# Up projection by two-by-two blocks with seven products in a transformer step on one core

## The chip, the cores and the metric

The kernel runs on one core of a Trainium2 chip. The time is the device time of one execution in microseconds, the median of several runs. TensorE (PE) multiplies, VectorE (DVE) and ScalarE (ACT) do elementwise work, GpSimd (POOL) and SyncE (SP) here only issue DMAs. SP's and ScalarE's DMAs are made by hardware queues, GpSimd's by a software queue; all run on the core's 16 DMA engines.

## What is computed

Two layers of a transformer trunk on 128 context tokens and 512 latent tokens, width 1024, float32. All tokens go through the kernel together as T = 644 columns (128 + 512 and four zero columns that pad the convolutions).

```python
def layer(l, x, cvec, ctx_kv, ang):
    m = (silu(cvec) @ w_mod[l] + b_mod[l])
    sh1, sc1, g1, sh2, sc2, g2 = split(m, 6)
    h = _rmsnorm(x, norm1_g[l]) * (1 + sc1) + sh1
    q, k, v, bg, cg, xc = split(h @ w_in[l], SPLITS)
    ...
    o = _diff_attention(q, k_all, v_all, lam)
    y = _rmsnorm(bg * _dwconv3(cg * xc, conv_w[l]), conv_norm_g[l])
    x = x + g1 * (concatenate([o, y]) @ w_out[l])
    h2 = _rmsnorm(x, norm2_g[l]) * (1 + sc2) + sh2
    a, b = split(_dwconv3(h2 @ w_up[l], ffn_conv_w[l]), 2)   # w_up: 1024 x 5632
    x = x + g2 * ((silu(a) * b) @ w_down[l])                 # w_down: 2816 x 1024
    return x, k, v
```

## The kernel before

Activations are kept transposed, features on the 128 partitions and tokens along the columns. Every large product of float32 values a and w is made of three matmuls at the fast float32r rate: both are split into a high part and the rest (h_hi, h_lo and w_hi, w_lo), and hi x hi, hi x lo and lo x hi are summed in PSUM. A weight unit is loaded by SP into raw (two slots of 2048 elements a partition), ScalarE copies it to w_hi (`split_hi`), VectorE subtracts to w_lo (`split_lo`), and TensorE uses it. The stages of a layer are: q/k/v projection (`qkv_unit`, columns in units of 256, T in tiles of 128 tokens as the stationary operand), gated convolution with the attention in between (`conv_half`), output projection (`out_unit`), and the MLP.

The MLP has 22 gates. A gate is a tile of 128 columns of the first half of w_up and the same of the second (a and b). `up_half` makes one half of the 644 columns (322) of one gate: 8 k tiles x 2 (a, b) x 3 matmuls into two PSUM banks. A gate has four banks, two gates alternate over all eight. `up_post` then takes them: ScalarE copies PSUM to ub and the centre tap to cen (which is tmp), VectorE adds the outer two taps, ScalarE makes silu, VectorE the product gt, ScalarE g_hi, VectorE g_lo. The gates are done in two chunks of 12 and 10 (`CHUNKS`); after each chunk the down projection (`down`) multiplies its gates by the rows of w_down that belong to them and VectorE adds the result to x (`add_to_x`, line 1491). Before the MLP the row sums of squares are made (`stat`), the inverse root is spread over the partitions by TensorE (`spread`), and VectorE and ScalarE make h_hi and h_lo of the normalised x (`norm_part`, `norm_hi`). The first gates follow this k tile by k tile.

The modulation vectors come from `mod_sum` (eight groups of small matmuls on a 1 MB unit of w_mod) and `mod_turn`; they are laid between the other work, where TensorE would wait.

The order on each engine is written out by hand and held by semaphores: each engine runs its own program in order. SP's order of loads is a list (`load_order`) up to the first gates, then loops; each load waits until the slot's last reader is done.

Of the kernel before, what the change touches and what calls it, by code (L numbers as in the profile page):

```python
# [7 lines left out]
F32 = mybir.dt.float32  # L8
# [4 lines left out]
ds = bass.ds  # L13
# [27 lines left out]
B_RMS = [(5, 6), (5, 6), (3, 5)]  # L41
# [8 lines left out]
CHUNKS = [12, 10]  # L50
CH0 = [0, 12]
C_U, O_U = 6, 12
UP_U = [16, 36]
DN_U = [28, 46]
N_SPLIT = 54
SPLIT_SLOT = N_SPLIT // 2
MOD_PRE = 8
MOD_LAYER = 24
RAW_SLOT = (N_SPLIT + MOD_LAYER) // 2
# [3 lines left out]
NORM1, MIXN, NORM2 = NT * KT, 2 * 4, 2 * KT  # L63
NORMED = NORM1 + MIXN + NORM2
# [5 lines left out]
GAP_H = [10] * LAST + [7]  # L70


def load_order(l):

    mod = [("mod", j) for j in range(MOD_LAYER)]
    split = [("split", n) for n in range(UP_U[0] + 2)]
# [4 lines left out]
    if l == LAST:  # L81
        return order + mod[12:14] + split[14:17] + mod[14:16] + split[17:18]
# [8 lines left out]
def raw_of(l, n):  # L91

    if n < UP_U[0] + 2:
        return ORDER[l].index(("split", n))
    if l == LAST:
        return n + MOD_LAYER - 8
    return n + MOD_LAYER - (2 if n < DN_U[0] + 2 else 0)


def mod_raw(l, j):  # L100

    return ORDER[l].index(("mod", j)) if j < MOD_LAYER - 2 else raw_of(l, DN_U[0] + 1) + 1 + j - (MOD_LAYER - 2)


# [8 lines left out]
YT_BANKS = [2, 3, 6, 7, 0, 1, 4, 5, 2, 3]  # L113
YT_WAITS = {0: 4, 4: 7, NT: KT}
# [5 lines left out]
def mod_bank(l, h):  # L120

    return PRE_BANKS[h] if l is None else MOD_BANK
# [5 lines left out]
def hybrid_step(nc, x_prompt, x_sample, cache_k, cache_v, c_sample, c_ctx, w_mod, b_mod, norm1_g, w_in, q_norm_g,  # L128
# [3 lines left out]
    with ctx:  # L132
# [18 lines left out]
        aT = sb("aT", [P, N_KEY])  # L151
# [9 lines left out]
        rope_q = sb("rope_q", [P, 2, 2, 4, HD])  # L161
# [33 lines left out]
        setup = ExitStack()  # L195
# [6 lines left out]
        g_hi = sb("g_hi", [P, CHUNKS[0] * T], F32R, scope=mlp)  # L202
        g_lo = sb("g_lo", [P, CHUNKS[0] * T], F32R, scope=mlp)
# [4 lines left out]
        vrow = sb("vrow", [P, DEPTH, 3, P], scope=setup)  # L208
        crow = sb("crow", [P, P], scope=setup)
# [219 lines left out]
        def _(pe):  # L429
# [111 lines left out]
            for l in range(DEPTH):  # L541
# [5 lines left out]
                def qkv_unit(b, t, c0, signal, follow=False):  # L547
# [13 lines left out]
                    elif signal:  # L561
                        ins.then_inc(qkv_full, 1)
# [1061 lines left out]
```

## Time and profile before

| | |
|---|---|
| median of 3 runs | 1702.11 us (1701.38 to 1702.33) |
| profiled execution | 1700.29 us, span of its instructions 1698.3 us |
| granted TensorE clock, mean | 0.981 |
| TensorE busy | 1650.8 us, 97% |
| VectorE busy | 894.3 us, 53% |
| ScalarE busy | 640.1 us, 38% |
| matmuls | 11763 |
| DMA | 162.75 MB, 95 GB/s over the span |

Matmul times overlap (a matmul's row gives 310 ns while the next starts after 148), so what one costs is read from the distance of starts, or from a window's count. The stages of layer 0 lie at about 53 to 162 us (q/k/v), 162 to 312 (convolution and attention), 312 to 392 (output projection), 392 to 568 (up, 12 gates), 568 to 657 (down), 657 to 800 (up, 10 gates), 800 to 872 (down); layer 1 follows in the same order from 876.

### The profile page before, as it was taken

What the parts mean: (1) busy time and instruction counts of PE and PEld (TensorE: products, weight loads), DVE (VectorE), ACT (ScalarE), POOL (GpSimd) and SP (SyncE); (2) the same over time, 40 slices, a digit from 0 to 9 for tenths busy, and PEclk for the clock granted to TensorE, in tenths of its full rate; (3) what the DMA queues carried; (4) which work ended last, traced back from release to release, by engine and by line L of the source; (5) the groups of instructions that cost most, each with busy time, mean ns of one, the idle gap of its engine ahead of it and who ended that gap; (6) DMA issues with size and microseconds to landing.
All of it is one profiled execution on the core that took longest, in us unless ns stands there. A gap on an engine that the chain in (4) does not pass through costs nothing.

```text
span 1698.3 us, 27158 instructions
## 1 busy us (share of the span) xinstructions
PE 1650.8 (97%) x11763; PEld 1580.6 (93%) x11763; DVE 894.3 (53%) x1484; ACT 640.1 (38%) x1015; POOL 4.7 (0%) x12
## 2 busy tenths in 40 slices
PE   5999999999999999999999999999999999999998
PEld 4799888988999999999989988889899999999998
DVE  4773666636655423554458547675655543255442
ACT  3543454324444312444234444442344431144432
POOL 0000000000000000000000000000000000000000
PEclk7899999998999999999989999999999999999999
DMA  9455110363322323221235531103322212322122
GB/s 329 147 181 178 36 50 26 97 209 93 100 75 63 102 85 89 73 73 37 78 112 174 181 106 50 51 26 124 100 75 75 69 57 75 100 75 75 47 65 76
DMA packets 225799, 162.75 MB, mean 96 GB/s; under 512 B 5456, under 2 KB 223120, under 8 KB 225680
## 3 DMA queue, kind: packets, MB, share of 16 engines
q1 hardware_dynamic: 224192, 158.36, 29.7%
q8 instruction: 93, 1.52, 0.4%
q0 software_dynamic: 640, 2.10, 0.3%
q10 hardware_dynamic: 848, 0.56, 0.1%
q14 instruction: 26, 0.21, 0.0%
HBM read 157.32 MB, written 3.67 MB: 95 GB/s over the span
## 4 chain that ended last, share of the span: by engine, by line
PE 90%; DVE 4%; ACT 2%; DMA 1%; issue 1%; DVEq 1%; SPq 0%; ACTq 0%
PE ps L776 12%; PE ps L777 12%; PE ps L778 12%; PE ps L822 6%; PE ps L823 6%; PE ps L824 6%; PE ps L556 3%; PE ps L558 3%; PE ps L557 3%; PE ps L455 3%; PE ps L437 3%; PE ps L438 3%; PE ps L439 3%; PE ps L713 2%; PE ps L647 2%; PE ps L714 2%
## 5 line engine op out<-in xcount | busy, mean ns | idle before, releaser
L776 PE MATMUL ps<-h_hi,w_hi 128*128 128x322 f32 x1408 | 440.3, 313 | 5.5 <-DVE h_lo L1301 5.4
L777 PE MATMUL ps<-h_lo,w_hi 128*128 128x322 f32 x1408 | 440.0, 312 | 0.0
L778 PE MATMUL ps<-h_hi,w_lo 128*128 128x322 f32 x1408 | 438.5, 311 | 0.0
L1260 DVE TENSOR_TENSOR w_lo<-raw,w_hi 128x2048 fp32r<-128x2048 f32 (+2 forms) x108 | 226.1, 2094 | 275.3 <-ACT w_hi L932 275.3
L932 ACT ACTIVATE w_hi<-raw 128x2048 fp32r<-128x2048 f32 (+2 forms) x108 | 189.8, 1758 | 358.8 <-PE ps L824 198.8
L776 PEld LDWEIGHTS ps<-h_hi,w_hi 128*128 128x128 f32 x1408 | 267.1, 190 | 6.3 <-issue 5.7
L778 PEld LDWEIGHTS ps<-h_hi,w_lo 128*128 128x128 f32 x1408 | 267.3, 190 | 0.0
L777 PEld LDWEIGHTS ps<-h_lo,w_hi 128*128 128x128 f32 x1408 | 266.9, 190 | 0.0
L822 PE MATMUL ps<-g_hi,w_hi 128*128 128x322 f32 x704 | 219.0, 311 | 0.9 <-DVE w_lo L1260 0.9
L823 PE MATMUL ps<-g_lo,w_hi 128*128 128x322 f32 x704 | 219.2, 311 | 0.0
L824 PE MATMUL ps<-g_hi,w_lo 128*128 128x322 f32 x704 | 219.0, 311 | 0.0
L1538 DVE SCALAR_TENSOR_TENSOR tmp<-ub,vecs,tmp 128x642 f32<-128x642 f32 x176 | 148.4, 884 | 61.3 <-ACT tmp L1111 58.0
L1491 DVE SCALAR_TENSOR_TENSOR x<-ps,modv,x 128x128 f32<-128x128 f32 x144 | 54.6, 435 | 204.2 <-PE ps L824 167.9
L556 PE MATMUL ps<-w_hi,h_hi 128*128 128x256 f32 x480 | 140.5, 293 | 4.5 <-DVE h_lo L1301 4.5
L557 PE MATMUL ps<-w_lo,h_hi 128*128 128x256 f32 x480 | 136.3, 284 | 0.0
L558 PE MATMUL ps<-w_hi,h_lo 128*128 128x256 f32 x480 | 136.3, 284 | 0.0
L822 PEld LDWEIGHTS ps<-g_hi,w_hi 128*128 128x128 f32 x704 | 132.9, 189 | 2.3 <-DVE w_lo L1260 1.5
L824 PEld LDWEIGHTS ps<-g_hi,w_lo 128*128 128x128 f32 x704 | 132.7, 189 | 0.0
L823 PEld LDWEIGHTS ps<-g_lo,w_hi 128*128 128x128 f32 x704 | 132.7, 188 | 0.0
L437 PE MATMUL ps<-h_hi,w_hi 128*128 128x322 f32 x384 | 123.6, 322 | 0.0
L438 PE MATMUL ps<-h_lo,w_hi 128*128 128x322 f32 x384 | 119.7, 312 | 0.0
L439 PE MATMUL ps<-h_hi,w_lo 128*128 128x322 f32 x384 | 119.1, 310 | 0.0
(158 smaller groups left out, 2318.3 us busy)
## 6 DMA issues: line engine op xcount, KB each, us to landing
raw<-in_w_up_dram SPq DMA_DIRECT2D x88, 512.0 KB, 4.7
raw<-in_w_mod_dram SPq DMA_DIRECT2D x80, 512.0 KB, 4.3
raw<-in_w_in_dram SPq DMA_DIRECT2D x48, 512.0 KB, 4.4
raw<-in_w_down_dram SPq DMA_DIRECT2D x32, 384.0 KB, 4.1
raw<-in_w_down_dram SPq DMA_DIRECT2D x32, 320.0 KB, 3.5
raw<-in_w_out_dram SPq DMA_DIRECT2D x16, 512.0 KB, 4.4
pre_w<-in_w_mod_dram SPq DMA_DIRECT2D x8, 512.0 KB, 10.0
pre_h<-in_w_mod_dram SPq DMA_DIRECT2D x8, 512.0 KB, 8.2
```

Of the source, the lines that this page charges most:

```text
L437: mm(out, wh[:, k, col:col + P], mov_hi(k), start=k == 0, stop=False)
L556: mm(out, h_hi[:, k, col:col + P], wh[:, k, :], start=k == 0, stop=False)
L557: mm(out, h_hi[:, k, col:col + P], wl[:, k, :], start=False, stop=False)
L558: ins = mm(out, h_lo[:, k, col:col + P], wh[:, k, :], start=False, stop=k == KT - 1)
L776: mm(out, w[0][s][:, k, :], hh, start=k == 0, stop=False)
L777: mm(out, w[0][s][:, k, :], hl, start=False, stop=False)
L778: ins = mm(out, w[1][s][:, k, :], hh, start=False, stop=k == KT - 1)
L822: mm(out, wh[:, k, :], gh, start=k == 0, stop=False)
L823: mm(out, wh[:, k, :], gl, start=False, stop=False)
L824: ins = mm(out, wl[:, k, :], gh, start=False, stop=k == kf - 1)
L932: A(w_hi[:, b, 0:size], raw[:, b, 0:size], ACT.Copy).then_inc(hi_done[b], 1)
L1260: V.tensor_tensor(w_lo[:, b, 0:size], raw[:, b, 0:size], w_hi[:, b, 0:size].bitcast(F32), ALU.subtract).then_inc(split_full[b], 1)
```

## The change

**Up projection.** The matrix of activations h2 (1024 x 644) is cut into two by two blocks: features in two halves of four k tiles, columns in two halves of 322. The weights of a gate are cut likewise into a and b, and first and second half of the features. Seven products of blocks replace eight (Winograd's form): the operands are B11, B12, B21, B22 and four combinations T1 to T4 of the activations, made once a layer (T4 takes B12's place), each with a weight block or a combination of weight blocks. In the code's numbering, product i uses raw block i: 0 holds A11, 1 the sum A21 + A22, 2 the sum of block 1 and A11 with its sign taken care of later, 3 holds A12, 4 the sum A21 + A11, 5 the sum of block 2 and A12, and a 7th block A22, which changes between places 6 and 7. Signs are taken up by the activations' combinations and by the scale of -1 where PSUM is read. Some products add into a bank that already holds others; in between, ScalarE takes copies of the bank (s1, p5, u2: `snapshot`), and VectorE puts the outputs together (c11, c22, c12), ScalarE c21. Gates 0 and 1 of each layer stay in the old form (`gate_tile`), the other 20 take seven products (`up_gate`).

**Weight sums.** SP loads seven blocks of 128 x 512 elements (256 KB) a gate; A11, A12 and A21 or their parts are loaded twice. GpSimd issues four DMAs that add one block of raw to another in SBUF (`add_block`, accumulate), each after its two operands have landed; ScalarE's w_hi copies wait for them.

**Chunks.** The down projection is done in four chunks of 6, 6, 5 and 5 gates; its weights come in four quarters of 256 columns.

**Normalisation before the MLP.** VectorE multiplies x by the spread inverse root, ScalarE applies gain and bias twice for each k tile, to hb_hi and to a full copy hfull from which the combinations are made. One pair of modulation sums gets a place of its own (mod_x) and is taken between the spread and the first gate.

**q/k/v.** A weight unit is now 512 columns of half of the k tiles; the matmuls have 512 columns instead of 256, and half their number.

```diff
-CHUNKS = [12, 10]
-CH0 = [0, 12]
+QC, KH = 512, KT // 2
+N_GATE, N_CLASSIC = FF // P, 2
+CHUNKS = [6, 6, 5, 5]
+CH0 = [0, 6, 12, 17]
+BLK = KH * P
+DW = 2 * P
...
+                def add_block(dst, src):
+
+                    pool.dma_start(raw_f[:, BLK * dst:BLK * (dst + 1)], raw_f[:, BLK * src:BLK * (src + 1)],
+                                   accum_op=ALU.add).then_inc(sum_full[dst], 16)
+
+                for g in range(N_CLASSIC, N_GATE):
+                    a22 = a22_block(g)
+                    pool.wait_ge(blk_full[a22], loaded(l, g, a22))
+                    pool.wait_ge(blk_full[1], loaded(l, g, 1))
+                    add_block(1, a22)
+                    pool.wait_ge(sum_full[1], summed(l, g))
+                    pool.wait_ge(blk_full[2], loaded(l, g, 2))
+                    add_block(2, 1)
+                    pool.wait_ge(blk_full[0], loaded(l, g, 0))
+                    pool.wait_ge(blk_full[4], loaded(l, g, 4))
+                    add_block(4, 0)
+                    pool.wait_ge(sum_full[2], summed(l, g))
+                    pool.wait_ge(blk_full[5], loaded(l, g, 5))
+                    add_block(5, 2)
...
-                    out = ps[:, t, c0:c0 + UC]
-                    for k in range(KT):
+                    out = ps[:, t, :]
+                    for i in range(KH):
+                        k = b * KH + i
                         if follow:
...
-                        mm(out, h_hi[:, k, col:col + P], wh[:, k, :], start=k == 0, stop=False)
-                        mm(out, h_hi[:, k, col:col + P], wl[:, k, :], start=False, stop=False)
-                        ins = mm(out, h_lo[:, k, col:col + P], wh[:, k, :], start=False, stop=k == KT - 1)
+                        mm(out, h_hi[:, k, col:col + P], wh[:, i, :], start=k == 0, stop=False)
+                        mm(out, h_hi[:, k, col:col + P], wl[:, i, :], start=False, stop=False)
+                        ins = mm(out, h_lo[:, k, col:col + P], wh[:, i, :], start=False, stop=k == KT - 1)
...
+                def up_gate(g):
...
+                    product(0, B11, bx, True)
...
+                    product(1, T1, by, True)
+                    pe.wait_ge(s1_ready, n + 1)
+                    pe.wait_ge(up_lo[1], n + 1)
...
+                    product(2, T2, bx, False)
...
+                    product(3, B21, bz, True)
+                    pe.wait_ge(u2_ready, n + 1)
+                    pe.wait_ge(up_lo[2], n + 1)
...
+                    product(4, T3, bx, False)
+                    pe.wait_ge(p5_ready, n + 1)
+                    product(5, B22, by, False)
+                    pe.wait_ge(c22_ready, n + 1)
+                    pe.wait_ge(up_lo[3], n + 1)
...
+                    product(6, T4, bx, False)
```

VectorE, one up gate in the middle of a chunk, before (w_lo is the split of the next weights, tmp the taps):

```order
L1260 TENSOR_TENSOR w_lo<-raw,w_hi 128x2048 [waits hi_done0]
L1538 SCALAR_TENSOR_TENSOR tmp<-ub,vecs,tmp 128x642 [waits up_read]
L1538 SCALAR_TENSOR_TENSOR tmp<-ub,vecs,tmp 128x642 x3
L1548 TENSOR_TENSOR gt<-tmp 128x644 [waits silu_ready]
L1552 TENSOR_TENSOR g_lo<-gt,g_hi 128x644 [waits gh_ready]
```

and of the change, one seven-product gate, where ub is put together from PSUM and s1, p5 and u2:

```order
L1869 SCALAR_TENSOR_TENSOR tmp<-ub,vecs,tmp 128x642 [waits cen_ready]
L1895 TENSOR_TENSOR w_lo<-raw,w_hi 128x512 [waits up_hi3]
L1869 SCALAR_TENSOR_TENSOR tmp<-ub,vecs,tmp 128x642
L1869 SCALAR_TENSOR_TENSOR tmp<-ub,vecs,tmp 128x642 [waits cen_ready]
L1895 TENSOR_TENSOR w_lo<-raw,w_hi 128x1024 [waits up_hi0]
L1869 SCALAR_TENSOR_TENSOR tmp<-ub,vecs,tmp 128x642
L1881 TENSOR_TENSOR gt<-tmp 128x644 [waits gh_ready,taps_ready,silu_ready]
L1910 TENSOR_TENSOR ub<-ps,s 128x322 [waits s1_ready,prod_done]
L1895 TENSOR_TENSOR w_lo<-raw,w_hi 128x1024 [waits up_hi1]
L1918 SCALAR_TENSOR_TENSOR ub<-ps,p 128x322 [waits p5_ready,prod_done]
L1887 TENSOR_TENSOR gg<-gt,gg 128x644 [waits gh_ready]
L1927 TENSOR_TENSOR ub<-ps,u 128x322 [waits u2_ready,prod_done]
L1895 TENSOR_TENSOR w_lo<-raw,w_hi 128x1024 [waits up_hi2]
```

One instruction that split the weights has become four, laid between the taps of the gate before and the three sums of this gate.

SyncE, the loads of two up gates before, each pair one gate:

```order
L336 DMA raw<-in_w_up_dram 128x8x128 [waits mod_used]
L336 DMA raw<-in_w_up_dram 128x8x128
L336 DMA raw<-in_w_up_dram 128x8x128 [waits split_full1]
L336 DMA raw<-in_w_up_dram 128x8x128
```

and of the change, the seven loads of one gate:

```order
L458 DMA raw<-in_w_up_dram 128x4x128 [waits up_lo3]
L458 DMA raw<-in_w_up_dram 128x4x128 [waits sum_full4,sum_full2,up_lo0]
L458 DMA raw<-in_w_up_dram 128x4x128
L458 DMA raw<-in_w_up_dram 128x4x128 [waits sum_full5,up_lo1]
L458 DMA raw<-in_w_up_dram 128x4x128
L458 DMA raw<-in_w_up_dram 128x4x128 [waits up_lo2]
L458 DMA raw<-in_w_up_dram 128x4x128
```

GpSimd, of the change, the sums of one gate, where nothing stood before:

```order
L548 DMA raw<-raw 128x512 [waits blk_full1,blk_full7]
L548 DMA raw<-raw 128x512 [waits blk_full2,sum_full1]
L548 DMA raw<-raw 128x512 [waits blk_full4,blk_full0]
L548 DMA raw<-raw 128x512 [waits blk_full5,sum_full2]
```

A load now waits for the splits of the gate before and for the sums that read its place, and the sums wait for loads and for one another.

## Rows read from the trace of the kernel before

**Rows 1.** The page's head: span, busy time of each engine, granted clock in 40 slices.

```profile
span 1698.3 us, 27158 instructions
...
PE 1650.8 (97%) x11763; PEld 1580.6 (93%) x11763; DVE 894.3 (53%) x1484; ACT 640.1 (38%) x1015; POOL 4.7 (0%) x12
...
PEclk7899999998999999999989999999999999999999
```

**Rows 2.** The page's chain that ended last, shares by engine.

```profile
PE 90%; DVE 4%; ACT 2%; DMA 1%; issue 1%; DVEq 1%; SPq 0%; ACTq 0%
```

**Rows 3.** Whom TensorE waited for: total us, times, longest.

```profile
PE ps L466 <- ACT mod_row L885: 8.3, 4, 6.2
PE ps L776 <- DVE h_lo L1301: 5.4, 2, 2.7
```

**Rows 4.** Windows: length, busy time of each engine, granted clock, DMA share, GB/s.

```profile
394.60:400.40 5.80, 5.80 (x22) 5.80 (x23) 5.52 (x19) 3.52 (x10) 0.00 (x0) 0.50 0.38 114
...
1440.00:1600.00 160.00, 160.00 (x1079) 160.00 (x1079) 71.23 (x72) 54.09 (x52) 0.00 (x0) 1.00 0.25 75
```

**Rows 5.** Timeline of TensorE in the q/k/v stage: start, us, what.

```profile
63.07 0.28 PE L557 MATMUL ps<-w_lo,h_hi 128*128 128x256 f32 x1
...
68.49 0.28 PE L558 MATMUL ps<-w_hi,h_lo 128*128 128x256 f32 x1
```

**Rows 6.** Groups by line and shape: count, busy us, mean ns, idle before.

```profile
L1260 DVE TENSOR_TENSOR w_lo<-raw,w_hi 128x2048 fp32r<-128x2048 f32 x76 | 174.1, 2291 | 267.6 <-ACT w_hi L932 267.6
L1538 DVE SCALAR_TENSOR_TENSOR tmp<-ub,vecs,tmp 128x642 f32<-128x642 f32 x176 | 148.4, 884 | 61.3 <-ACT tmp L1111 58.0
L932 ACT ACTIVATE w_hi<-raw 128x2048 fp32r<-128x2048 f32 x76 | 145.5, 1915 | 196.0 <-PE ps L778 151.0 <-PE ps L824 36.0 <-PE ps L558 9.0
...
L1552 DVE TENSOR_TENSOR g_lo<-gt,g_hi 128x644 fp32r<-128x644 f32 x44 | 36.5, 829 | 35.6 <-ACT g_hi L1119 35.6
...
L1117 ACT ACTIVATE tmp<-tmp 128x644 f32<-128x644 f32 x44 | 32.7, 744 | 141.9 <-DVE tmp L1538 141.9
...
L1491 DVE SCALAR_TENSOR_TENSOR x<-ps,modv,x 128x320 f32<-128x320 f32 x48 | 26.1, 543 | 0.0
...
L1260 DVE TENSOR_TENSOR w_lo<-raw,w_hi 128x1280 fp32r<-128x1280 f32 x16 | 23.9, 1491 | 2.8 <-ACT w_hi L932 2.8
...
L932 ACT ACTIVATE w_hi<-raw 128x1280 fp32r<-128x1280 f32 x16 | 20.4, 1278 | 71.8 <-PE ps L824 71.8
...
L988 ACT ACTIVATE qraw<-ps 128x512 f32<-128x512 f32 x20 | 11.9, 595 | 2.5 <-DVE qn L1376 2.5
```

**Rows 7.** Timeline at the first up gate of layer 0: TensorE, then ScalarE.

```profile
386.79 3.58 PE L455 MATMUL ps<-raw,cT 128*32 128x256 f32 x32
390.29 1.60 PE L487 MATMUL ps<-sq,ones 128*128 128x128 f32 x12
394.60 0.61 PE L776 MATMUL ps<-h_hi,w_hi 128*128 128x322 f32 x1 [2.70 <-DVE h_lo L1301]
...
392.14 2.66 ACT L950 ACTIVATE h_hi<-tmp,modv 128x128 fp32r<-128x128 f32 x8 [1.11 <-DVE tmp L1292]
```

**Rows 8.** DMA: the software queue's packets, MB, share; issues, KB each, median us to landing.

```profile
q0 software_dynamic: 640, 2.10, 0.3%
...
raw<-in_w_up_dram SPq DMA_DIRECT2D x88, 512.0 KB, 4.7
...
out_dram<-qn POOLq DMA_DIRECT2D x2, 256.0 KB, 5.3
out_dram<-v POOLq DMA_DIRECT2D x2, 256.0 KB, 2.4
```

**Rows 9.** Timeline of DMA issues of SyncE and GpSimd in the q/k/v stage.

```profile
116.43 0.92 SPq L293 DMA_DIRECT2D raw<-in_w_in_dram  x2
...
117.95 0.55 POOL L417 DMA_DIRECT2D out_dram<-qn  x1 [76.82 <-DVE qn L1363]
```

More of the change, by code:

```diff
@@ L81, in load_order @@
     if l == LAST:
-        return order + mod[12:14] + split[14:17] + mod[14:16] + split[17:18]
+        return order + split[14:17] + mod[12:14] + split[17:18]
     for h in range(6, 9):
@@ L221, in hybrid_step @@
         xf = x[:, :, :].rearrange("p t n -> p (t n)")
+        raw_f, whi_f, wlo_f = (t[:, :, :].rearrange("p b n -> p (b n)") for t in (raw, w_hi, w_lo))
+        hb_hi, hb_lo = (t[:, :, :, :].rearrange("p k s n -> p k (s n)") for t in (hc_hi, hc_lo))
+        hfv = hfull[:, :, :].rearrange("p k (h n) -> p k h n", h=2)
         mf = modv[:, :, :, :].rearrange("p v t s -> p (v t s)")
@@ new lines, in _, with product @@
+                ins.then_inc(unit_done[1], 1)
+                def product(b, part, bank, first):
+                    out = ps[:, bank, 0:HALF]
+                    for k in range(KH):
+                        c0 = BLK * b + P * k
+                        mm(out, whi_f[:, c0:c0 + P], hc_hi[:, k, part, :], start=first and k == 0, stop=False,
+                           skip_group_check=not first)
+                        mm(out, whi_f[:, c0:c0 + P], hc_lo[:, k, part, :], start=False, stop=False,
+                           skip_group_check=not first)
+                        ins = mm(out, wlo_f[:, c0:c0 + P], hc_hi[:, k, part, :], start=False, stop=k == KH - 1,
+                                 skip_group_check=not first)
+                    ins.then_inc(prod_done, 1)
@@ L820, in down @@
+                def down(c, m, k0, k1):
+                    kf, b = CHUNKS[c], m // 2 % 2
+                    wh, wl = (half[:, b, 0:kf * DW].rearrange("p (t n) -> p t n", n=DW)[
+                        :, :, m % 2 * P:(m % 2 + 1) * P] for half in (w_hi, w_lo))
+                    for h in range(2):
+                        out = ps[:, down_banks(c, m)[h], 0:HALF]
                         for k in range(k0, k1):
-                            gh, gl = (g[:, k * T + h * HALF:k * T + (h + 1) * HALF] for g in (g_hi, g_lo))
+                            gh, gl = (gg[:, k, i, h * HALF:(h + 1) * HALF] for i in range(2))
@@ L1506, in _ @@
                     n = O_U + k // 2
[L1507 removed]
+                    if k % 2 == 0 and k and l < LAST:
                         mod_post(l, 5 + k // 2)
```

919 lines of the change are left out of this document (619 added, 300 removed).

## Prediction

> **What bounds the kernel now.** I read the page's head first, then the chain that ended last, who the tensor engine waited for, and the stages in windows. TensorE is busy 97% of the span, VectorE 53%, ScalarE 38% [rows 1]; the chain that ended last is 90% TensorE [rows 2]; TensorE's longest waits for another engine after the start-up are 2.7 us, one for each layer's first up gate [rows 3]. In the 160 us from 1440, all up projection and its down projection, TensorE is never idle, at the full granted clock (2.4 GHz level), and starts 1079 matmuls: 0.1483 us each [rows 4]. So a removed 322-column matmul is worth 0.148 us, as long as nothing else becomes late. The weight DMAs there take 25% of the 16 engines at 75 GB/s.
>
> **What is removed.** Before, a gate tile (128 columns of each half of w_up) takes 8 x 2 x 2 x 3 = 96 matmuls. By seven products of four k tiles it takes 7 x 4 x 3 = 84. Two gates of each layer stay as they were, 20 change: 2 x 20 x 12 = 480 matmuls fewer, all on the path: 480 x 0.1483 = **-71.2 us**. The down projection keeps its 2112. In q/k/v, 1440 matmuls of 256 columns become 720 of 512. Two 256s cost 0.236 us: from 63.07 to 68.49 us there are 46 intervals of 0.118 [rows 5]. No row has a 512-column matmul of this kind. The two widths shown (0.118 at 256, 0.1483 at 322) lie on a line through nearly zero, which puts 512 at 0.237; if instead what each takes above columns/2.4 GHz (11 and 14 ns) stays 14 ns, it is 0.228, and with nothing above it 0.213. So this edit is worth between 0 and 720 x 0.023 = 16 us; I take 0, since the two rows that exist scale with the columns. The Trainium skill ("TensorE: Matmul & The Clock Gate", Back-to-back issue gap) gives N/2.4 + 2.5 ns, 216 ns for 512. The trace disagrees with it at both widths (109 and 137 ns by the rule, 118 and 148 here); by it this edit would give 720 x 0.020 = 14 us.
>
> **What the seven products ask of VectorE and ScalarE.** A product is 12 matmuls, 1.78 us; a gate 12.46 us (14.2 before). VectorE per gate: w_lo for 3 x 1024 and 512 elements; from the 2048 and 1280 forms (2.29 and 1.49 us) 1024 takes 1.22 and 512 takes 0.69; four taps of 0.88, gt and the low part of g 0.83 each, and three new sums that read 322 columns of PSUM, priced as the 320-column update, 0.54 each [rows 6]: 11.2 us of 12.46. ScalarE: 3 x 1.07 + 0.64 for w_hi, four PSUM reads of about 0.45 (512 columns take 0.60), four passes over 644 of 0.74: 8.6 us. Both fit, VectorE with little left, so its order matters. The tightest wait in the written order is that of the seventh product (c22_ready): the fourth product ends at 7.12 us, then ScalarE's w_hi 1.07, VectorE's w_lo 1.22 and the c22 sum 0.54 end at 9.95, about 10.3 with the hand-offs; TensorE comes there at 10.68. It holds by 0.4 us. In the two six-gate chunks of a layer the last gate has a 1536-element split for the down weights there (1.76 instead of 1.22) and misses by 0.5 us; with small waits where the down chunks start, **+3 us** in all. The softer work (down_add, twice as many passes over x, about 1.3 us for each 4.5 or 5.3 us of matmuls) hides under down matmuls.
>
> **The start of each MLP.** Before, TensorE idles 2.70 us between the spread and the first gate [rows 7]; then 5.8 us of matmuls run at the 1.2 GHz level [rows 4]. Now two modulation sums, moved from elsewhere, fill the gap (3.58 us for two in rows 7): about -2.5. ScalarE then makes four passes for each k tile, 2 x (0.33 + 0.60) = 1.9 us against TensorE's 1.78, and gate 1 waits for w_lo (2.29): this comes out as before, within 0.5. Then VectorE has four 1288-element sums and three low parts (1.5 to 1.8 each), four taps and a split before the first seven-product gate: 16 us beside 14.2 of TensorE, late by 1.6; the fourth low part and the gate's own work delay its c22 by 3.4 more. Net +2.5 for each layer, **+5 us**.
>
> **The weight sums by DMA.** This is what the trace cannot settle. The weights of a gate are now seven 256 KB blocks from HBM, three of them loaded twice, and four accumulating SBUF to SBUF transfers issued by GpSimd. Traffic: 7 x 262 KB in 12.46 us is 147 GB/s; at 75 GB/s for 0.25 [rows 4] that is half of the DMA engines. GpSimd's eight transfers took 0.3% of 16 engines' span [rows 8], 0.64 us each; with the destination read as well up to 1.3, so four sums add 20 to 40%. The engines hold it, but the latencies are in series. Call A the time from a sum's issue to its landing. Bounds: a GpSimd store of the same 256 KB lands after 2.4 us when the queue is empty, and after 5.3 us when it is issued 1.5 us behind two weight loads of 512 KB [rows 8, 9]; a second read may add 0.6. So A lies between 2.4 and 5.9. At most two 256 KB blocks are in flight beside a sum, half of that load, so I take A = 4.0. A lone block takes 2.0 us and a pair 2.9 (4.7 us for 1 MB [rows 8], less the bytes at 300 GB/s). The loop: up_lo[2] frees blocks 4 and 5; load 2.0; sum into 4, A; that frees block 0 for the next gate; load pair 2.9; sum into 1, A; sum into 2, A; sum into 5, A; w_hi 1.07, w_lo 1.22, hand-offs 0.3. That is 7.5 + 4A for two gates, which have 24.9 us. It holds up to A = 4.35; at 4.0 there is 0.7 us to spare a gate, and some gates will miss: **+6 us**, an estimate. A late sum holds ScalarE's w_hi copy, and behind it in ScalarE's order the low-priority gate work (g_hi, then c21 of this gate), behind that VectorE's w_lo and c22, and then TensorE. Beyond 4.35 each of the 24 gates that are not first or second in their chunk pays (7.5 + 4A - 24.9)/2: the down projection covers the first two. The Trainium skill ("DMA: Bandwidth & Descriptors", Anatomy of one DMA) fits 2.0 us + bytes/436e3, 2.6 us for such a transfer, and says (Queues, rings and completion order) that a DMA engine takes turns between rings at every packet. By that no gate would wait and the sum would be 6 us lower; the trace speaks against the turn-taking, with 5.3 us against 2.4.
>
> **The sum.** Profiled execution 1700.3 us (span 1698.3 and 2.0 around it), 1.8 below the median of 1702.1. 1700.3 - 71.2 + 3 + 5 + 6 = 1643; with the 1.8, **1645 us**.
>
> **Rivals.**
> (a) *The 512-column matmuls are cheaper than two of 256.* For: a fixed part for each matmul is usual. Against: the two widths scale. 1645 - 14 = 1631; 12%.
> (b) *The DMA loop binds mildly*, A about 5: 12 x 2 x 2.6/2 = 31 us in place of 6: 1670. For: the 5.3 us row. 20%.
> (c) *The DMA loop binds hard and the kernel is slower than before.* Place: the sum into block 2 and then block 5, each waiting in GpSimd's queue for the one before. The gain net of the starts is 63 us; it is used up where 12 x (4A - 17.4) = 63, at A = 5.7. At A = 6.5 it costs 103 us: 1742. For: adding may be slower than copying by more than a second read, and the loads it competes with have doubled. Against: 5.7 needs nearly all of the upper bound of 5.9. 13%.
> (d) *VectorE's order binds*: c22 later than reckoned by 0.8 us, 0.4 us a gate over 40 gates, 16 us: 1661; 6%.
> The forecast's case, 1636 to 1655, has 49%.
>
> **How the numbers follow.** Range 1624 to 1700: low end from (a) with 16 us and fewer missed gates, high end with A = 5.5 and part of (d); (c) is left out. A measurement of this kernel tells apart about 0.2%, 3.4 us. Forecast, (a), (b), (d) are all faster: 87%, of which 2% I give to ending within 0.2%; slower 13%.
>
> **What would show it.** Right: matmuls of 322 columns fewer by 480; TensorE busy over 97%; seven-product gates 12.5 us apart; sums by GpSimd landing in 3.5 to 4.4 us; 512-column matmuls 0.23 to 0.24 apart; q/k/v stage as long as before; TensorE waits of 1 to 3 us at each layer's first seven-product gate. Wrong: w_hi on ScalarE waiting for the raw blocks in most gates, with gates 13 us or more apart (b, c); the seventh product waiting on the c22 sum in each gate (d); the q/k/v stages shorter by 7 us each (a). It would be most wrong if an accumulating transfer took much longer than a plain one.

## The result: slower than before, and outside the forecast range

The changed kernel takes 1713.67 us (median of 4 runs, 1713.11 to 1714.50) against 1701.79 us for the kernel before beside it (4 runs, 1701.38 to 1702.33). The ratio is 1.0070, with a 95% interval of 1.0053 to 1.0087: slower by 0.7%. The forecast was 1645, with a range up to 1700. The sign is wrong, and 69 us are to be explained.

The page of the changed kernel, its head and the granted clock, to set beside [rows 1]:

```profile
span 1711.7 us, 26600 instructions
## 1 busy us (share of the span) xinstructions
PE 1600.2 (93%) x10563; PEld 1479.9 (86%) x10563; DVE 1061.9 (62%) x1778; ACT 739.1 (43%) x1275; POOL 143.4 (8%) x172
...
DMA  9455011372856846758425531113175685584762
...
q1 hardware_dynamic: 259584, 189.82, 35.6%
q0 software_dynamic: 23680, 44.05, 14.6%
```

TensorE's share fell from 97% to 93%: the matmuls are gone, and waits stand in their place. The software queue, 0.3% of the DMA engines before [rows 8], has 14.6%. Whom TensorE waited for (us in total, times, longest), against 2.7 us as the longest wait for an up gate before [rows 3]:

```profile
PE ps L953 <- ACT u L1389: 32.7, 23, 3.2
PE ps L953 <- DVE ub L1918: 15.2, 19, 1.7
...
PE ps L953 <- DVE w_lo L1895: 5.6, 2, 3.1
```

L953 is the first matmul line of a product. Its 23 waits for `u` are waits ahead of a gate's fifth product (the T3 product, which waits for u2_ready), for ScalarE's snapshot of PSUM; the 19 for `ub` are waits ahead of the seventh product, for c22. Of all waits in the kernel, the rows on the weight sums:

```profile
POOL raw L548 <- DMA raw<-in_w_up_dram: 940.5, 56, 272.3
POOL raw L548 <- DMA raw<-raw: 186.6, 62, 5.8
...
ACT w_hi L1370 <- DMA raw<-raw: 145.9, 50, 5.6
```

The last row is the sign that the prediction named for its rivals (b) and (c): ScalarE's w_hi copy stands 50 times and 145.9 us for a sum in flight.

**Where the time went, by stages.** Lengths are from the start of a stage's first matmul to the start of the next stage's, in the two profiled executions (1698.3 and 1711.7 us, 13.4 apart).

| step of the prediction | forecast, us | measured, us | from |
|---|---|---|---|
| 480 matmuls fewer | -71.2 | -71.2 | an undisturbed gate is 12.45 to 12.46 |
| q/k/v in 512 columns | 0 | -1.3 | 108.56 to 107.52 and 107.85 to 107.64 |
| chunk ends, down projection | +3 | +4.2 | 170.8 to 172.4 and 157.7 to 157.5, and the 2.8 below; the last gate of every chunk is 12.45 |
| start of each MLP | +5 | +23.5 | below |
| loop of loads and sums | +6 | +61.2 | the 38 seven-product gates that are not first in a layer, above 12.46 each |

These give +16.4; the remaining -3.0 lies in stages that no step speaks of (the convolution stages are 1.3 shorter, the stretch behind the last down projection 1.5). The starts are three things in each layer: from the out projection to the first up gate 81.6 to 85.6 and 72.6 to 74.0; the two gates of twelve passes (each k tile of such a gate is twelve matmuls) 31.6 to 35.8 and 31.2 to 35.3; and the first seven-product gate, 19.0 and 18.6 instead of 12.46. Together that is 26.3, but 32 matmuls of modulation sums stand in layer 0's stretch ahead of the first gate that before stood in its first down projection. There they had cost 2.8 us: that stage took 88.5 us with them and 85.6 in layer 1 without, and the corresponding stages of the changed kernel, which have none, are equal. So the table counts 2.8 less for the starts and 2.8 more for the down projection.

**Which gates are long.** First gates of the later chunks are 12.45. The second ones of these chunks are 14.8 to 18.6, the middle ones mostly 14.0 to 15.3, the last ones 12.45 (behind them no next gate is loaded). In one ordinary gate of layer 0 (starts at 704.4, 14.8 us long) GpSimd, ScalarE and TensorE show the following (start, duration, what, idle time before it and what ended it):

```profile
696.42 1.74 POOL L548 DMA_DIRECT2D raw<-raw  x2 [4.53 <-DMA raw<-raw]
699.95 0.85 POOL L548 DMA_DIRECT2D raw<-raw  x1 [1.79 <-DMA raw<-raw]
705.67 0.86 POOL L548 DMA_DIRECT2D raw<-raw  x1 [4.87 <-DMA raw<-in_w_up_dram]
711.22 1.76 POOL L548 DMA_DIRECT2D raw<-raw  x2 [4.69 <-DMA raw<-raw]
```

```profile
701.11 5.87 SPq L458 DMA_DIRECT2D raw<-in_w_up_dram  x6
```

```profile
706.72 0.82 ACT L1330 ACTIVATE tmp<-ub,vecs 128x644 f32<-128x644 f32 x1
711.04 1.06 ACT L1370 ACTIVATE w_hi<-raw 128x1024 fp32r<-128x1024 f32 x1 [3.50 <-DMA raw<-raw]
712.00 0.42 ACT L1389 ACTIVATE p<-ps 128x322 f32<-128x322 f32 x1
712.32 0.43 ACT L1389 ACTIVATE u<-ps 128x322 f32<-128x322 f32 x1
```

```profile
712.81 0.42 PE L953 MATMUL ps<-hc_hi,w_hi 128*128 128x322 f32 x1 [1.12 <-ACT u L1389]
```

Read them as a ring. At 696.42 GpSimd issues sums 2 and 4 one behind the other, since sum 1 has landed. At 701.11, when sum 4 has landed, SyncE may overwrite block 0 and issues blocks 0 and 1 of the next gate. Block 1 is there at 705.67: sum 1. GpSimd then stands 4.69 us for sum 1, and at 711.22 issues sums 2 and 4 again. From 696.42 to 711.22 is 14.8 us, and the gate is 14.8 us long. The ring closes like this, each member issued within 1.2 us of the landing of the one before, 16 times; these turns take 14.2 to 15.6 us. ScalarE stands for the same sum 1 (3.50 us), its snapshots p and u stand behind that in its order, and TensorE stands for u. The prediction had this ring over two gates, 7.5 + 4A against 24.9 us; the trace has it in one gate.

### The profile page after: what moved, and what is told of

It is laid out like the page before. It is cut to its first block and busy times, and to the rows that moved or that the text cites. A ratio compares the mean times of both kernels' runs of the same rounds, so it can differ in the third digit from the quotient of the medians.

```text
span 1711.7 us, 26600 instructions
## 1 busy us (share of the span) xinstructions
PE 1600.2 (93%) x10563; PEld 1479.9 (86%) x10563; DVE 1061.9 (62%) x1778; ACT 739.1 (43%) x1275; POOL 143.4 (8%) x172
## 3 DMA queue, kind: packets, MB, share of 16 engines
q0 software_dynamic: 23680, 44.05, 14.6%
## 5 line engine op out<-in xcount | busy, mean ns | idle before, releaser
L953 PE MATMUL ps<-hc_hi,w_hi 128*128 128x322 f32 x1120 | 358.0, 320 | 55.2 <-ACT u L1389 32.7
L955 PE MATMUL ps<-hc_lo,w_hi 128*128 128x322 f32 x1120 | 353.4, 316 | 0.0
L957 PE MATMUL ps<-hc_hi,w_lo 128*128 128x322 f32 x1120 | 352.7, 315 | 0.0
L953 PEld LDWEIGHTS ps<-hc_hi,w_hi 128*128 128x128 f32 x1120 | 215.6, 193 | 68.0 <-ACT u L1389 39.4
L1370 ACT ACTIVATE w_hi<-raw 128x1024 fp32r<-128x1024 f32 x120 | 126.5, 1059 | 321.0 <-DMA raw<-raw 145.9
L1010 PE MATMUL ps<-gg,w_hi 128*128 128x322 f32 x704 | 219.2, 311 | 0.7 <-DVE gg L1887 0.7
L1011 PE MATMUL ps<-gg,w_hi 128*128 128x322 f32 x704 | 218.9, 311 | 0.0
L1012 PE MATMUL ps<-gg,w_lo 128*128 128x322 f32 x704 | 218.4, 310 | 0.0
L955 PEld LDWEIGHTS ps<-hc_lo,w_hi 128*128 128x128 f32 x1120 | 215.7, 193 | 0.0
L1010 PEld LDWEIGHTS ps<-gg,w_hi 128*128 128x128 f32 x704 | 132.5, 188 | 1.8 <-DVE gg L1887 1.8
L1011 PEld LDWEIGHTS ps<-gg,w_hi 128*128 128x128 f32 x704 | 133.0, 189 | 0.0
L582 PE MATMUL ps<-h_hi,w_hi 128*128 128x322 f32 x384 | 122.7, 320 | 0.0
L583 PE MATMUL ps<-h_lo,w_hi 128*128 128x322 f32 x384 | 119.5, 311 | 0.0
L584 PE MATMUL ps<-h_hi,w_lo 128*128 128x322 f32 x384 | 118.9, 310 | 0.0
## 6 DMA issues: line engine op xcount, KB each, us to landing
pre_w<-in_w_mod_dram SPq DMA_DIRECT2D x8, 512.0 KB, 10.1
```

Of the source, the lines that this page charges most:

```text
L582: mm(out, wh[:, k, col:col + P], mov_hi(k), start=k == 0, stop=False)
L583: mm(out, wh[:, k, col:col + P], mov_lo(k), start=False, stop=False)
L953: mm(out, whi_f[:, c0:c0 + P], hc_hi[:, k, part, :], start=first and k == 0, stop=False, skip_group_check=not first)
L955: mm(out, whi_f[:, c0:c0 + P], hc_lo[:, k, part, :], start=False, stop=False, skip_group_check=not first)
L957: ins = mm(out, wlo_f[:, c0:c0 + P], hc_hi[:, k, part, :], start=False, stop=k == KH - 1, skip_group_check=not first)
L1010: mm(out, wh[:, k, :], gh, start=k == 0, stop=False)
```

## Experiments

A "seven-product sum" below is the length of all 40 seven-product gates; 40 x 12.46 is 498.4, and in the changed kernel it is 572.3. The ratios are to the kernel before, run on the same chip, with 95% intervals. The runs came in four groups, in which the median of the kernel before was 1698.5, 1700.4, 1698.7 and 1698.7.

### Break the ring at block 1

```
                         sp.wait_ge(up_lo[0], n)
                         sp.wait_ge(sum_full[2], summed(l, g - 1))
+                        block(1, 1, 0, g)
                         sp.wait_ge(sum_full[4], summed(l, g - 1))
...
                     block(0, 0, 0, g)
-                    block(1, 1, 0, g)
+                    if not i:
+                        block(1, 1, 0, g)
```

> The changed kernel, with one wait moved in SyncE's order: block 1 of the next gate is loaded once sum 2 has landed and its place is split, and only block 0 waits for sum 4 as well. Theory A (the sums' loop of latencies binds: sum 4 landed, load of blocks 0 and 1 4.0 us, sum 1 4.7, sum 2 and sum 4 issued 0.8, sum 4 4.1, which makes the 14.5 us between gates): block 1 starts 1.5 us earlier, gates in the middle of a chunk come down from 14.5 to about 13, and the kernel from 1714 to 1670 to 1685 us. Rival B (the order of ScalarE and VectorE within a gate binds, whatever the DMAs do): 1710 to 1716. Rival C (the DMA engines' throughput binds, 75 to 85% busy): within 5 us of 1714.

1664.28 us (1663.50 to 1667.78), ratio 0.9801 (0.9780 to 0.9823). The seven-product sum fell from 572.3 to 525.1. Nothing was removed: the same loads, the same sums. What it moved is one load out of the ring, past one semaphore. The gates that are not the first of a layer are now 18 us above 12.46 in sum, where they were 61. So at least 43 of the 61 us were latencies in series and not the throughput of the DMA engines, whose share in the 160 us from 1440 went up as the time went down. This is the first of several versions that are faster than both kernels. Windows of the changed kernel, then of this one (length, busy time of PE, PEld, DVE, ACT, POOL, granted clock, DMA share, GB/s), which answer to the second row of [rows 4]:

```profile
1440.00:1600.00 160.00, 154.89 (x1034) 153.03 (x1033) 95.33 (x138) 60.98 (x83) 22.51 (x26) 1.00 0.61 151
```

```profile
1440.00:1600.00 160.00, 156.80 (x1050) 155.35 (x1049) 105.96 (x146) 74.05 (x109) 30.97 (x36) 1.00 0.75 176
```

What was left in it, TensorE's waits in the gates:

```profile
PE ps L955 <- DVE ub L1920: 15.3, 17, 1.6
...
PE ps L955 <- DVE w_lo L1897: 4.8, 2, 2.6
```

### Leave the sums out

```
-                for g in range(N_CLASSIC, N_GATE):     # GpSimd's sums
+                for g in range(0):
```

ScalarE's waits for a sum become waits for its block, and SyncE's waits for sums are left out.

> The changed kernel without the weight sums: GpSimd's 160 adding transfers and all waits on them are left out, so the products use plain weight blocks (that part of the computation is left out); the 280 block loads, splits, products and sums of outputs stay. Theory A or C: all 40 seven-product gates take 12.5 us, 74 us less, so about 1640 us. Rival B: gates stay at 13.5 us or more, 1680 us or more.

1645.10 us (1644.26 to 1648.32), ratio 0.9688 (0.9667 to 0.9709). Every seven-product gate is 12.45 to 12.46 us but the first of each layer (16.5, 17.5) and the one behind the second of these (12.96). So VectorE's and ScalarE's orders hold in the steady state: c22 ends 0.6 us (median) ahead of the seventh product, where the prediction gave it 0.4. Rival (d) falls with this. That the figure equals the forecast is chance: the forecast held 6 us of loop that are absent here, and the starts cost more than its 5.

### Copy instead of add

```
-                                   accum_op=ALU.add).then_inc(sum_full[dst], 16)
+                                   ).then_inc(sum_full[dst], 16)
```

> The changed kernel with plain copies of the same blocks in place of the adding transfers (the additions are left out), same queue, order and waits. It prices the adding alone. Expected by theory A: a copy lands 0.6 to 1 us earlier than a sum (no read of the destination, issue 0.55 us instead of 0.92), the loop has three of them, so gates near 12.5 to 13 us and 1650 to 1680 us. By rival B 1710 or more. If the adding costs nothing, and only the latency of any software DMA counts, 1705 to 1714.

1649.78 us (1644.96 to 1650.03), ratio 0.9703 (0.9677 to 0.9728). The seven-product sum is 12.2 us above 498.4, of which 3.5 are in gates that are not the first of a layer. The ring is the same; its two GpSimd members are shorter (medians 2.7 and 2.5 us), and the pair of loads a little (3.7). By these medians one turn takes about 10 us, an estimate, well below a gate's 12.46. The line of the sums, first in the changed kernel and then with copies (duration of the issue in ns, min/median/max; at the end, issue to landing in us):

```profile
L548 POOL DMA_DIRECT2D raw<-raw x160: 845/862/1217, 421.2 to 1648.9; - x160
...
DMA to landing us min/median/max: 3.2/3.8/6.4
```

```profile
L548 POOL DMA_DIRECT2D raw<-raw x160: 536/536/545, 420.8 to 1582.7; - x160
...
DMA to landing us min/median/max: 2.2/2.5/5.0
```

Adding costs 1.3 us of landing and 0.33 us of issue over a copy of the same 256 KB.

### Sum 4 ahead of sum 2, in the changed kernel

```
                     add_block(1, a22)
+                    pool.wait_ge(blk_full[0], loaded(l, g, 0))
+                    pool.wait_ge(blk_full[4], loaded(l, g, 4))
+                    add_block(4, 0)
                     pool.wait_ge(sum_full[1], summed(l, g))
                     pool.wait_ge(blk_full[2], loaded(l, g, 2))
                     add_block(2, 1)
-                    pool.wait_ge(blk_full[0], loaded(l, g, 0))
-                    pool.wait_ge(blk_full[4], loaded(l, g, 4))
-                    add_block(4, 0)
```

> The changed kernel with one edit: GpSimd issues the four sums of a gate as 1, 4, 2, 5 instead of 1, 2, 4, 5. Theory A (the loop of one gate: load of block 0 4.0 us, sum 1 4.7, then sum 4, which stands behind sum 2 in GpSimd's order, 4.1): sum 4 is issued when block 4 and sum 1 are there, 6.0 us into a gate instead of 6.8, so the loop is 0.8 to 1 us shorter in some 28 gates: 1685 to 1698. Theory B (ScalarE's and VectorE's order alone sets the gate): no change, 1710 to 1717. Theory C (the DMA engines are out of throughput): the same bytes move, no change, 1710 to 1717; a later sum 2 and sum 5 could even make it longer.

1793.63 us (1790.33 to 1798.49), ratio 1.0561 (1.0530 to 1.0592): none of the three had this. Whom TensorE waited for, and GpSimd over one gate:

```profile
PE ps L953 <- DVE ub L1918: 84.6, 30, 4.4
...
PE ps L953 <- ACT u L1389: 7.3, 6, 2.2
```

```profile
606.45 0.86 POOL L548 DMA_DIRECT2D raw<-raw  x1 [4.62 <-DMA raw<-in_w_up_dram]
612.93 1.75 POOL L548 DMA_DIRECT2D raw<-raw  x2 [5.61 <-DMA raw<-in_w_up_dram]
617.83 0.85 POOL L548 DMA_DIRECT2D raw<-raw  x1 [3.15 <-DMA raw<-raw]
```

The waits for u, the mark of the first ring, fell from 32.7 to 7.3. But GpSimd now stands 5.61 us for block 4, with sum 2 behind it in its order. The next gate's block 4 can only be loaded when this gate's blocks 4 and 5 have been split, which waits for the sixth product of the gate before. In a gate of 16.7 us (the one from 590.0) the load is issued at 1.7 and lands at 5.6, sums 4 and 2 are issued at 6.1 and 6.6, sum 2 lands at 10.7, and w_hi (1.06), w_lo (1.23) and c22 (0.48) end at 13.5; TensorE was ready for its seventh product at 10.7. The next gate starts when that product ends. This is a new ring, through TensorE itself. The expectation reckoned sum 2's delay and left out what reads it.

The same order of sums in a kernel with the first ring already broken:

> The kernel e6_order with GpSimd's order 1, 4, 2, 5. With the first loop out of the way, sum 4 early gains nothing; sums 2 and 5 land some 2 us later in the gate, at about 10.4 and 14.7 us after its start, which are wanted by the third and fifth product of the next gate, 3.6 and 7.1 us into it: the same as e6_order within 2 us. If the loop of blocks 2 and 5 binds, it is slower than e6_order by 5 to 25 us.

1759.15 us (1757.36 to 1767.68), ratio 1.0366 (1.0333 to 1.0399), 84 us above the kernel that it was made from (next section), where 0 or 5 to 25 had been expected. The size was far off. The cause is the same: outside the first gates of the chunks sum 4 is issued 0.53 us behind the landing of block 4 in 31 of 32 gates, and sum 2 0.5 to 0.8 behind sum 4. TensorE's largest wait, 74.2 us in 30 times, is for the snapshot s.

### What holds the rest: c22's place or a second ring

Two edits of order to the 1664 kernel. The first moves ScalarE's snapshots ahead of its w_hi copy, VectorE's next split back by one step and c22 forward:

```
+                        snapshot(g, p5, by, 2, c22_ready, p5_ready)
+                        snapshot(g, u2, bx, 3, c12_ready, u2_ready)
                         if nxt is not None:
                             up_split_hi(nxt, 0)
-                        snapshot(g, p5, by, 2, c22_ready, p5_ready)
-                        snapshot(g, u2, bx, 3, c12_ready, u2_ready)
...
                             taps(prev, 1, 0)
-                            if nxt is not None:
-                                up_split_lo(nxt, 0)
...
                             gate_mult(prev)
+                            if nxt is not None:
+                                up_split_lo(nxt, 0)
                         c11(g)
+                        c22(g)
                         if nxt is not None:
                             up_split_lo(nxt, 1)
                         else:
                             down_split_lo(c, 0)
-                        c22(g)
```

> The kernel with block 1 loaded early (1664) and besides two changes of order: ScalarE takes the two snapshots of PSUM (p5, u2) ahead of the copy of the next gate's first weight pair, and VectorE makes the next gate's w_lo one step later, c22 ahead of the second of them. Left in the 1664 kernel are 17 waits of TensorE for c22, 15.3 us in all. If these come from the written order (theory D), they go: 1647 to 1652, near the 1645 of the kernel without sums. If they come from the DMA loop of blocks 2 and 5 (block 2 3.4 us, sum 2 3.8, sum 5 4.2, and 1 us between, about 12.5 us a gate), which no order of the engines can shorten, TensorE waits at another product instead: 1660 to 1665.

1674.83 us (1669.36 to 1675.75), ratio 0.9853 (0.9827 to 0.9878). The second moves c22 alone:

> The kernel with block 1 loaded early (1664), and VectorE takes c22 ahead of the split of the next gate's second weight pair (or of the down weights); nothing else is moved, above all not the split that frees block 1, which e6_order moved back by 1.9 us. Theory: what e6_order lost was that split: up_lo[0], load of block 1, sums 1, 2 and 5 in a row, ScalarE's w_hi for the fifth product, and behind it the snapshot that the third product of the next gate waits for. Without that, the 15.3 us of waits for c22 go and none comes: 1647 to 1654. Rival: sums 2 and 5 are so late that TensorE finds another wait wherever VectorE stands: 1660 to 1670.

1667.65 us (1666.37 to 1668.65), ratio 0.9818 (0.9791 to 0.9845): the rival's range in both cases. TensorE's waits in the gates, of the first and of the second:

```profile
PE ps L955 <- ACT s L1391: 20.2, 18, 1.6
```

```profile
PE ps L955 <- ACT s L1391: 18.6, 19, 2.3
```

The waits for c22 are gone (in the first kernel but for 2.7 us) and as many for `s`, ahead of the third product, have come. The seven-product sums are 525.1, 529.8 and 525.4 for the three orders: a different product waits and the length stays. This is a ring again: block 2 may be overwritten when sum 5 has read it. By the landing times of the second kernel (medians) block 2's load takes 3.8, sum 2 3.8, sum 5 4.2, and the hand-offs between them 0.53, 0.28 and 0.06: 12.7 us, against 12.46. In 14 of its gates the ring is closed, that is, each member is issued by such a hand-off behind the landing of the one before; these turns take 12.9 to 15.0 us, with a median of 13.8. ScalarE stands for sum 5 in its order ahead of the snapshot s:

```profile
570.90 1.06 ACT L1372 ACTIVATE w_hi<-raw 128x1024 fp32r<-128x1024 f32 x1 [2.88 <-DMA raw<-raw]
571.87 0.42 ACT L1319 ACTIVATE ub<-ps 128x322 f32<-128x322 f32 x1
572.19 0.82 ACT L1332 ACTIVATE tmp<-ub,vecs 128x644 f32<-128x644 f32 x1
572.91 0.62 ACT L1361 ACTIVATE w_hi<-raw 128x512 fp32r<-128x512 f32 x1
573.43 0.42 ACT L1391 ACTIVATE s<-ps 128x322 f32<-128x322 f32 x1
```

The counterpart is the same edit in the changed kernel, where the first ring is intact:

> The changed kernel, and VectorE takes c22 ahead of the split of the next gate's second weight pair. TensorE waited for c22 19 times there, 15.2 us in all. Theory A (the loop of block 0 sets the length of a middle gate, about 14.4 us): the wait moves to the fourth product and the time stays, 1708 to 1714. Rival B (each wait is a loss of its own, made by the written order): 1696 to 1700.

1716.73 us (1714.15 to 1723.69), ratio 1.0113 (1.0077 to 1.0150): no gain, as the ring says, and 3 us above where it was expected. The 15.2 us of waits for c22 went over to u:

```profile
PE ps L953 <- ACT u L1389: 46.9, 26, 3.0
```

So an engine's wait in the list is not a price. Here some 13 to 15 us of waits were removed three times, and three times nothing was gained.

### The start of the MLP

In the changed kernel, from the out projection's end, ScalarE and VectorE (start, duration, what, idle before):

```profile
391.25 1.91 ACT L1118 ACTIVATE w_hi<-raw 128x2048 fp32r<-128x2048 f32 x1 [5.77 <-DMA raw<-in_w_up_dram]
393.07 0.58 ACT L1069 ACTIVATE mod_row<-ps 128x512 f32<-128x512 f32 x1
393.54 1.19 ACT L1282 ACTIVATE hc_hi<-hfull,modv,gain 128x128 fp32r<-128x128 f32 x2
...
394.63 1.19 ACT L1285 ACTIVATE hfull<-hfull,modv,gain 128x128 f32<-128x128 f32 x2
```

and TensorE, which was done with the spread and with the second pair of modulation sums by 390.2:

```profile
393.70 1.02 PE L614 MATMUL ps<-ident,mod_row 128*128 128x128 f32 x4 [3.49 <-ACT mod_row L1069]
396.83 0.60 PE L930 MATMUL ps<-hc_hi,w_hi 128*128 128x322 f32 x1 [2.11 <-DVE hc_lo L1852]
```

The modulation sums are ready, but the row read stands behind the weight copy of gate 1, which waits 5.77 us for its load. The edit, on top of the first of the two order kernels and then of the second:

```
-                split_hi(G_U + 1)
                 rows(l, GAP_A[l])
                 for k in range(KT):
+                    if k == 1:
+                        split_hi(G_U + 1)
```

> The kernel e6_order with one more change at the start of each MLP: ScalarE reads the modulation row before it copies the weights of gate 1 (1.91 us, after a wait for their load), and not after. The first scaled k tile waits for that row in both layers. Theory: it comes 2 us earlier in each layer, so 3 to 4 us less than e6_order. Rival: the first k tile is held by VectorE's products x times rms, or by the DMA of gate 0, and nothing moves (within 1 us).

1668.34 us (1664.85 to 1670.91), 6.5 below the kernel that it was made from; ratio 0.9818 (0.9790 to 0.9847).

> The kernel e9_c22, and at the start of each MLP ScalarE reads the modulation row before it copies the weights of gate 1. In e8_start that made the first gate start 2 to 3 us earlier and the two twelve-pass gates 2 us longer, since ScalarE's four passes for a k tile (2.2 us) set their pace: 0 to 2 us less than e9_c22.

1660.89 us (1660.13 to 1661.10), 6.8 below; ratio **0.9779** (0.9747 to 0.9810). This is the fastest version, 2.2% below the kernel before and, by the two ratios, 2.9% below the change as made. From the first q/k/v matmul to the first seven-product gate the traces give 2.8 and 1.1 us less in the first pair, 2.0 and 2.5 in the second: 4.0 and 4.4 us, the first expectation's size and twice the second's. The other 2 to 3 us were not placed; the start-up ahead of the first q/k/v matmul differs by as much between profiles, and of the first pair the two profiled executions are only 0.5 us apart.

### Adds on GpSimd itself

```
-                    pool.dma_start(raw_f[:, BLK * dst:BLK * (dst + 1)], raw_f[:, BLK * src:BLK * (src + 1)],
-                                   accum_op=ALU.add).then_inc(sum_full[dst], 16)
+                    nc.gpsimd.tensor_tensor(raw_f[:, BLK * dst:BLK * (dst + 1)], raw_f[:, BLK * dst:BLK * (dst + 1)],
+                                            raw_f[:, BLK * src:BLK * (src + 1)], ALU.add
+                                            ).then_inc(sum_full[dst], 16)
```

> The kernel e10_c22_start, and GpSimd makes the four sums of a gate itself, 512 elements a partition each, instead of issuing a transfer for each. The output is the same. Left in e10_c22_start are 26.6 us above 40 x 12.46 in the seven-product gates, 8 of them in the first gate of each layer. Theory A (latency of transfers in series, two loops: block 0 with sums 1 and 4, block 2 with sums 2 and 5): an add takes GpSimd 0.7 (VectorE's time for 512 elements) to 2 us in place of 3.2 to 6 us, both loops come far below a gate, all waits but the first gates' go: 1638 to 1646. Rival: GpSimd's adds slow VectorE's own operations, which fill 11.2 of a gate's 12.46 us, by at least 1.5 us a gate: 1665 or more.

1694.36 us (median of 11, 1691.44 to 1708.87), ratio 0.9974 (0.9964 to 0.9984): 33 us worse than the version that it was made from. The rival held. The profiled execution is the longest of the eleven (1708.87), so the groups are to be compared, not its span. GpSimd's line (ns, min/median/max):

```profile
L550 POOL TENSOR_TENSOR raw<-raw x160: 1277/1524/2631, 422.8 to 1639.6; 128x512 f32<-128x512 f32 x160
```

and VectorE's groups, with adding transfers (the 1660.9 version) and then with GpSimd's adds:

```profile
L1872 DVE SCALAR_TENSOR_TENSOR tmp<-ub,vecs,tmp 128x642 f32<-128x642 f32 x176 | 151.3, 884 | 21.2 <-ACT tmp L1333 14.3
L1898 DVE TENSOR_TENSOR w_lo<-raw,w_hi 128x1024 fp32r<-128x1024 f32 x120 | 146.6, 1222 | 139.8 <-ACT w_hi L1373 139.7
```

```profile
L1873 DVE SCALAR_TENSOR_TENSOR tmp<-ub,vecs,tmp 128x642 f32<-128x642 f32 x176 | 203.3, 1177 | 30.4 <-ACT tmp L1334 23.5
L1899 DVE TENSOR_TENSOR w_lo<-raw,w_hi 128x1024 fp32r<-128x1024 f32 x120 | 175.4, 1462 | 65.6 <-ACT w_hi L1374 65.5
...
L1914 DVE TENSOR_TENSOR ub<-ps,s 128x322 f32<-128x322 f32 x40 | 19.5, 487 | 7.5 <-PE ps L960 7.5
```

The latency part of the theory was right: ScalarE waits for sums twice, 2.9 us in all. But a tap went from 884 to 1177 ns, a 1024-element split from 1222 to 1462, the 512-element one from 684 to 874, the low part of g from 823 to 1197. Per gate that is 4 x 0.29 + 3 x 0.24 + 0.19 + 0.37 = 2.4 us on top of VectorE's 11.2, 13.6 against 12.46. The sums that read one operand from PSUM did not change (487 ns in both). Taken one by one, with no add beside them and with one beside more than half of their time (medians): a tap 0.89 and 1.92 us, a 1024-element split 1.22 and 2.31, the low part of g 0.82 and 1.92, a sum from PSUM 0.49 and 0.49. The product gt has two SBUF operands too and stayed at 829 ns, but no add ran beside it for that long. The Trainium skill ("GPSIMD Engine Reference", the table of its specifications) says that GpSimd's SBUF interfaces are shared with VectorE and contend with instructions that have two SBUF inputs; the rows agree, in which operations slowed and in which did not.

## Why the prediction was wrong, step by step

**Right.** *The matmuls.* 0.148 us each, 12.46 us a gate; without the sums 37 of 40 gates have that length. *q/k/v.* 512-column matmuls start 0.23 us apart, as named, and the stage keeps its length. The 512-column units alone, put into the kernel before:

> The kernel before with the q/k/v part of the change alone: 512-column matmuls on weight units of half of the k tiles. The prediction's value is 0 (two 256-column matmuls 0.236 us, one of 512 0.237): 1700 to 1704 us. From the changed kernel's trace, where 512-column matmuls start 0.233 us apart and the stage is 1.1 and 0.3 us shorter: 1699 to 1701. By a fixed part for each matmul 1688.

1696.12 us (median of 11, 1694.68 to 1701.64), ratio 0.9992 (0.9979 to 1.0005). The row's reading held against the -14 us that the prediction worked out from the Trainium skill ("TensorE: Matmul & The Clock Gate", Back-to-back issue gap): here twice 256 columns (2 x 0.118) take as long as 512 (0.233, the median distance of starts). Two matmuls of that kind in it:

```profile
54.01 0.39 PE L558 MATMUL ps<-w_hi,h_hi 128*128 128x512 f32 x1
54.23 0.40 PE L559 MATMUL ps<-w_lo,h_hi 128*128 128x512 f32 x1
```

*Chunk ends.* +4.2 in place of +3, though the half-microsecond miss in the six-gate chunks, a part of that +3, did not occur. *The place of the risk.* The prediction named the loop of loads and sums as what the trace of before could not settle, and the wait by which to know it.

**Wrong: the loop, +61 for +6.** The step that failed is "7.5 + 4A for two gates". Its terms against the changed kernel's landings (medians): the load of block 4, which starts beside sum 1, 2.0 against 4.4; the pair 2.9 against 4.0; A 4.0 against 4.8, 3.3, 4.1 and 3.7 for sums 1, 2, 4 and 5. A was right on average, the loads were not. With the measured terms the two-gate formula gives 7.5 + 2.4 + 1.1 + 15.9 = 26.9 us against 24.9, 1 us a gate in 24 gates: that is 24 of the 61 us. The rest is put down to the ring's shape. The prediction freed block 0 by sum 4 and then let sum 1 follow once in two gates; in the code block 1 stands behind block 0 in SyncE's order, sum 4 behind sum 2 in GpSimd's, and each gate has its own sums 1 and 4. One turn of load 4.0, hand-off 0.6, sum 1 4.8, hand-off and the issue of sum 2 0.8 to 1.0 and sum 4 4.1 is 14.3 to 14.5 us, for every gate. The first experiment shows it, since it changes only which loads stand behind sum 4, and 18 of the 61 us were left. Two smaller parts of the step failed with it. "The down projection covers the first two gates": it covers one. The place of the second gate's block 4 comes free only inside the first gate: in one chunk its load is issued 2.5 us into that gate and its sum 4 lands at 10.1, so the third gate's block 0 is late, its sum 1, beside six loads, takes 6.0 us, and the second gate, at 16.7, is the one that waits. And ScalarE's snapshots were left out: they stand behind the w_hi copy of the next gate, so a late sum 1 stops TensorE a gate earlier than the next gate's own weights would.

**A second part of it: slow matmuls behind the waits.** Of the 73.9 us above 498.4, 57 are gaps and 17 are matmuls that start 0.2 to 0.33 us apart (some 150 of them). One place, around TensorE's wait of 3.20 us that ends at 790.63: granted clock 0.50, the 1.2 GHz level, in the window behind it, 13 matmuls in 3.0 us.

```profile
785.40:787.50 2.10, 2.03 (x14) 1.76 (x12) 0.00 (x0) 0.00 (x0) 0.00 (x0) 1.00 1.04 233
...
791.50:794.50 3.00, 3.00 (x13) 3.00 (x12) 2.91 (x4) 1.69 (x2) 0.85 (x1) 0.50 0.78 141
```

Behind the wait of 1.12 us at 712.81 the product took 1.89, behind the one of 3.20 us 3.38. In the kernel with sum 4 ahead of sum 2 the slow part is 48 us.

**Wrong: the starts, +23.5 for +5.** Three sizes. The idle gap ahead of the first gate was to be filled with moved modulation sums; it grew, since the first scaled k tile comes late: the modulation row stands behind a weight copy in ScalarE's order (+2.6 for both layers, the moved 2.8 taken off, forecast -5). The 32 moved matmuls fill 1.9 us of it, not the 3.58 that the prediction read for as many in rows 7. ScalarE's four passes for a k tile take 2.2 us (two passes 1.19 in the rows above, each pair starting 1.09 behind the last), not 1.9, and TensorE needs 1.78: the twelve-pass gates lose 4.2 and 4.1 us, forecast "within 0.5". The first seven-product gate loses 6.5 and 6.1, forecast 5.0; of that 4.0 and 5.0 remain without sums.

**The rivals.** (b) and (c) had the mechanism, and between them a third of the chance. Neither had the price right: (c) needed A = 5.7, and the kernel was slower at A = 3.8. The range left (c) out with 13%; it held the result.

**What stays open.** That the second ring sets the 525 us of the 1661 to 1675 versions rests on three orders with nearly one sum and on the closed turns; no version that keeps the adding transfers and breaks that ring alone was tried. In the fastest version 26.6 us are left above 498.4, 8 of them in the first gates of the layers.

## What to carry to other kernels

When buffers are refilled by transfers that depend on one another, write down, for each buffer, the ring from "free" to "free" again, including every instruction that stands ahead of each member in its queue, and compare its length with one period of the loop; a mean latency in a formula over two periods says little if the ring closes in one. An entry in a list of waits names who was last, not what the removal would bring: test it by looking for what is late next. And before an idle engine is given work, look at which operands its neighbour reads.

## What was not expected of the hardware

- An adding transfer of 256 KB within SBUF lands 3.8 us after its issue (3.2 to 6.4) and occupies its queue for 0.86; the copy takes 2.5 (2.2 to 5.0) and 0.54. The software queue's share of 14.6% of 1711.7 us, less the 0.3% of its eight other transfers, is 1.53 us of 16 engines for each adding transfer; the copies' (7.0% of 1648.2 us, likewise) is 0.69. The landing differs within the kernel: a gate's first sum takes 3.2 to 3.8 us in the first gates of the later chunks and 5.0 (median) from a chunk's third gate on.
- GpSimd's own add of 512 elements a partition takes 1.5 us, and VectorE's operations with two SBUF operands take 20 to 45% longer on average over gates that have four such adds, and 1.9 to 2.6 times as long beside one.
- Swapping two transfers in one queue cost 80 us (ratio 1.0561 against 1.0070), with every other instruction the same.
